# Score steps that keep a running minimum, differential values projected beside the step columns, and merged small products

## The reference, cut to what matters

```python
proj = h @ w_in[l]
a_q, a_k, a_v, b_z, b_xbc, b_dt, c_q, c_k, c_v = jnp.split(proj, offsets, axis=-1)
# windowed attention, 6 heads: softmax over scores and one sink logit per head
scores = jnp.einsum('bnqgrd,bnkgd->bngrqk', qb, kb) * (HEAD_DIM ** -0.5)
bias = -slopes * jnp.abs(rel)
scores = jnp.where(valid, scores + bias, -jnp.inf)
m = jnp.maximum(jnp.max(scores, axis=-1, keepdims=True), sink_l)
p = jnp.exp(scores - m)
denom = jnp.sum(p, axis=-1, keepdims=True) + jnp.exp(sink_l - m)
# differential attention, 4 heads of two maps each: 8 softmaxes
sc = jnp.einsum('bqhmd,bkhmd->bhmqk', qn, k) * (DIFF_QK_DIM ** -0.5)
a = jax.nn.softmax(sc - sl * dist, axis=-1)
attn = a[:, :, 0] - lam * a[:, :, 1]
# state-space mixer: b_dt goes through softplus, a running sum over tokens, and decays
dt = jax.nn.softplus(dt_raw + dt_bias)
da = jnp.cumsum(dt * a, axis=2)
y_diag = einsum(einsum(ch, bh) * decay, xdt)
```

## Time and profile before

| | before |
|---|---|
| median of 3 runs | 1211.71 us (1211.57 to 1214.07) |
| span of the profiled execution | 1213.5 us; its own time is not listed apart from the three above |
| TensorE / VectorE / ScalarE busy | 78% / 33% / 16% |
| moved by DMA | 436.64 MB, mean 360 GB/s |
| mean granted TensorE clock | 0.897 of 2.4 GHz |

### The profile page before, as it was taken

How to read it: one execution, slowest core, us unless ns; L and a number is a source line. 1 busy time by engine, 2 the same in 40 slices (tenths; PEclk the granted TensorE clock), 3 DMA queues, 4 the chain that set the end, 5 groups by cost and what they waited for, 6 DMA issues and landing times.

```text
span 1213.5 us, 26544 instructions
## 1 busy us (share of the span) xinstructions
PE 948.9 (78%) x11004; PEld 600.0 (49%) x11004; DVE 398.7 (33%) x1231; ACT 189.6 (16%) x546; POOL 8.9 (1%) x27
## 2 busy tenths in 40 slices
PE   7999989766668787895799999895666666666964
PEld 6877855433334443453387777553333333333532
DVE  4778453111122222231176774431111111111213
ACT  2245221000001110110023352110000000000101
POOL 2000000000000000000000000000000000000000
PEclk9999989888789998997899999898888888787977
DMA  9835179999999999999995244899999999999994
GB/s 342 334 123 209 70 296 425 424 427 427 426 424 424 426 426 425 400 425 428 408 394 199 97 182 156 344 426 426 425 428 426 426 427 427 425 425 426 424 423 196
DMA packets 47435, 436.64 MB, mean 360 GB/s; under 512 B 8256, under 2 KB 10304, under 8 KB 21440
## 3 DMA queue, kind: packets, MB, share of 16 engines
q1 hardware_dynamic: 47296, 434.72, 86.5%
HBM read 433.65 MB, written 1.05 MB: 358 GB/s over the span
## 4 chain that ended last, share of the span: by engine, by line
PE 47%; DMA 37%; DVE 6%; issue 5%; SPq 2%; DVEq 2%; ACT 1%; another core or an unknown queue 1%; ACTq 0%
DMA ring<-in_w_up 37%; PE ps L601 13%; PE ps L689 8%; PE ps L617 5%; PE ps L812 4%; PE ps L626 3%; PE ps L569 3%; PE ps L701 2%; PE ps L589 2%; PE ps L706 1%; PE ps L752 1%; SPq L442 1%; SPq L440 1%; PE ps L791 1%
## 5 line engine op out<-in xcount | busy, mean ns | idle before, releaser
L601 PE MATMUL ps<-ring,xg 128*32 128x256 f32 x4352 | 317.3, 455 | 176.9 <-DMA ring<-in_w_up 171.5
L601 PEld LDWEIGHTS ps<-ring,xg 128*32 128x32 f32 x4352 | 170.0, 130 | 307.3 <-issue 247.1
L1135 DVE SCALAR_TENSOR_TENSOR th<-th,ps 128x128 f32<-128x128 f32 x72 | 20.7, 288 | 593.8 <-ACT th L934 593.8
L617 PE MATMUL ps<-ring,actT 128*32 128x256 f32 x2304 | 139.2, 382 | 13.5 <-issue 12.8
L617 PEld LDWEIGHTS ps<-ring,actT 128*32 128x32 f32 x2304 | 69.0, 109 | 74.6 <-DVE actT L1139 22.3
L934 ACT ACTIVATE th<-ps 128x128 f32<-128x128 f32 x72 | 20.0, 278 | 515.7 <-PE ps L601 480.1
L569 PE MATMUL ps<-xh,Pb 128*32 128x256 f32 x1152 | 79.4, 394 | 24.5 <-issue 20.4
L689 PE MATMUL ps<-hT,ring 128*128 128x256 f32 x416 | 95.3, 386 | 0.8 <-ACT hT L971 0.8
L689 PEld LDWEIGHTS ps<-hT,ring 128*128 128x128 f32 x416 | 78.6, 193 | 12.7 <-issue 1.4
L626 PE MATMUL ps<-ysb,PwT 32*128 32x256 f32 x992 | 71.8, 403 | 0.0
L569 PEld LDWEIGHTS ps<-xh,Pb 128*32 128x32 f32 x1152 | 38.5, 113 | 49.3 <-issue 24.5
(11 more groups left out here) (251 smaller groups left out, 744.0 us busy)
## 6 DMA issues: line engine op xcount, KB each, us to landing
ring<-in_w_down SPq DMA_DIRECT2D x62, 2048.0 KB, 40.4
ring<-in_w_gate SPq DMA_DIRECT2D x60, 2048.0 KB, 45.6
ring<-in_w_up SPq DMA_DIRECT2D x60, 2048.0 KB, 47.3
ring<-in_w_in SPq DMA_DIRECT2D x6, 2048.0 KB, 19.8
ring<-in_w_out SPq DMA_DIRECT2D x4, 2048.0 KB, 19.5
ring<-in_w_gate SPq DMA_DIRECT2D x8, 1024.0 KB, 29.1
ring<-in_w_up SPq DMA_DIRECT2D x8, 1024.0 KB, 31.8
ring<-in_w_in SPq DMA_DIRECT2D x4, 1024.0 KB, 21.3
```

Source lines behind the costliest of these rows:

```text
L601: last = mm(b_gate[j * SLOTS:(j + 1) * SLOTS, 0:2 * GQ], tokens[:, k, :], ring[:, low:high + 1:high - low, o:o + GQ], start=(k == 0), stop ...
L617: last = mm(b_y[j * SLOTS:(j + 1) * SLOTS, 0:DQ], actT[:, c * SLOTS:(c + 1) * SLOTS], ring[:, slot, o:o + DQ], start=(c == 0), stop=(c == ...
```

## The change

1. **Scores.** The scale and the slope are put into the queries (`qscale`, one factor per partition, applied in the copies of `aq` and `cq`). `sc.u` on VectorE becomes two `tensor_tensor_reduce` instructions, one per 128 queries, each of which adds the distance table to the bank, multiplies by -slope and keeps the running minimum, started at the negated sink (or a large number). The exponential on ScalarE then uses scale -1 and that minimum as bias. The maxima and the scaling of them go away.
2. **Step columns beside differential values.** Input piece 1 now holds the last 128 columns of `xbc`, the 12 `dt` columns and the 256 columns of `c_v`, loaded by two DMAs; piece 4 holds `cq` and `ck`. The steps `dt` (TensorE part) and `cv` are replaced by `dc.0` and `dc.1`, one per 128 tokens, each 8 matmuls of 268 columns, placed where `dt` was. ScalarE copies them out with the norm factor; VectorE's `dt` starts from that copy.
3. **Merged products.** `cum` takes both token halves in one product, so 3 matmuls take the place of 6. `cb.0` and `cb.1` become one TensorE step `cB`, placed where `cb.0` was, whose four matmuls alternate between the two halves of the rows; ScalarE still copies `cb.0` and `cb.1` in their old places.

The bank planner runs over the new list. By its rule `pT.6` now gets bank 0 (it is the lower of two that tie), so `outA.0` waits for ScalarE's copy of `pT.6`; `outA.1` waits for VectorE's `sc.12`, and `outA.2` for `sc.10`.

```diff
-W_IN_PIECES = [(O_XBC, 512), (O_XBC + 512, O_CK - O_XBC - 512), (O_AQ, O_AV), (O_AV, O_XBC - O_AV), (O_CK, D_IN - O_CK)]
+W_IN_PIECES = [[(O_XBC, 512)], [(O_XBC + 512, O_CQ - O_XBC - 512), (O_CV, D_IN - O_CV)], [(O_AQ, O_AV)], [(O_AV, O_XBC - O_AV)],
+               [(O_CQ, O_CV - O_CQ)]]
+DC = 2 * S_H + C_H * C_V
 ORDER = """
...
-    dt conv.4 ak silu.3 aq.0 dta xs.0 silu.4 sc.0 nm.0 aq.2 xs.1 aS.0 cum cumT aq.1 lam cb.0 sc.1 sc.2 seg.0.0
+    dc.0 dc.1 dt conv.4 ak silu.3 aq.0 dta xs.0 silu.4 sc.0 nm.0 aq.2 xs.1 aS.0 cum cumT aq.1 lam cB cb.0 sc.1 sc.2 seg.0.0
...
-    pT.2 cq.1 sc.5 pT.3 y.5 sc.6 cS.0 sc.7 oa.0 nm.5 ybn pT.4 nm.6 cv oa.1 pT.5 yT.0 yT.1 oa.2 sc.8 sc.9 sc.10
+    pT.2 cq.1 sc.5 pT.3 y.5 sc.6 cS.0 sc.7 oa.0 nm.5 ybn pT.4 nm.6 oa.1 pT.5 yT.0 yT.1 oa.2 sc.8 sc.9 sc.10
     nm.7 pT.6 cS.1 sc.11 sc.12 outA.0 pT.7 outA.1 od.0 nm.8 sc.13 nm.9 pT.8 od.1 outA.2 pT.9 od.2 od.3 outA.3 ycn
...
+        return [("cb", g) for g in range(S_G)]
...
-                    elif kind == "dt":
+                    elif kind == "dc":
                         w = piece(piece_of(s), s)
+                        t = s[1]
+                        for k in range(KC):
+                            last = mm(bank[:, 0:DC], hT[:, k, t * P:(t + 1) * P], w[:, k, P:P + DC], start=(k == 0), stop=(k == KC - 1))
...
+                        sums = bank[:, 0:TT * 4 * S_H].rearrange("p (t n) -> p t n", t=TT)
+                        mm(sums[:, :, 0:S_H], upto[:, :], dta[:, :, 0:S_H], start=True, stop=True)
+                        mm(sums[:, :, S_H:2 * S_H], since[:, :], dta[:, :, S_H:2 * S_H], start=True, stop=True)
+                        last = mm(sums[:, :, 2 * S_H:4 * S_H], ones[:, :], dta[:, :, 0:2 * S_H], start=True, stop=True)
...
+                        for t in range(TT):
+                            for g in range(S_G):
+                                r = slice(g * S_N, (g + 1) * S_N)
+                                last = mm(ps[BANK["cb", g]][:, t * SEQ:(t + 1) * SEQ], xc[r, 3, t * P:(t + 1) * P], xc[r, 4, :],
+                                          start=True, stop=True)
...
+                        last = A(dcv[:, s[1], :], bank[:, 0:DC], ACT.Copy, scale=root[:, TT + s[1]:TT + s[1] + 1])
...
+                            last = A(pb[:, t, :], pb[:, t, :], ACT.Exp, bias=low[:, u, t:t + 1], scale=-1.0, accum_out=den[:, u, t:t + 1])
...
+                        dve.wait_ge(done["act"], nth(li, "act", ("dc", 0), ("dc", 1)))
+                        v.tensor_tensor(z.rearrange("p (t n) -> p t n", t=TT), dcv[:, :, 0:n],
+                                        rowp[:, R_DTB:R_DTB + n].unsqueeze(1).broadcast_to([P, TT, n]), ALU.add)
...
-                            v.scalar_tensor_tensor(pb[:, t, :], table[:, o:o + SEQ], slope, bank[:, t * SEQ:(t + 1) * SEQ],
-                                                   ALU.mult, ALU.add)
-                        dve.drain()
-                        v.reduce_max(nmx[:, 0, u, :], pb[:, :, :], AX_X)
-                        if u < A_H:
-                            dve.drain()
-                            last = v.tensor_scalar(nmx[:, 1, u, :], nmx[:, 0, u, :], -A_SCALE, nsink[:, HEAD[u]:HEAD[u] + 1],
-                                                   ALU.mult, ALU.min)
-                        else:
-                            dve.drain()
-                            last = v.tensor_scalar(nmx[:, 1, u, :], nmx[:, 0, u, :], -C_SCALE, None, ALU.mult)
+                            last = v.tensor_tensor_reduce(pb[:, t, :], bank[:, t * SEQ:(t + 1) * SEQ], table[:, o:o + SEQ], -slope, least,
+                                                          ALU.add, ALU.min, low[:, u, t:t + 1])
```

More of the change, by code:

```diff
@@ L140, in piece_of @@
         return len(W_IN_PIECES) + (kind == "outB")
-    return {"xbc": int(step[-1] == 4), "dt": 1, "cq": 1, "aq": 2, "ak": 2, "vz": 3, "ck": 4, "cv": 4}.get(kind)
+    return {"xbc": int(step[-1] == 4), "dc": 1, "aq": 2, "ak": 2, "vz": 3, "cq": 4, "ck": 4}.get(kind)
 USERS = [[step for step in COUNT["pe"] if piece_of(step) == n] for n in range(PIECES)]
@@ L687, in _ @@
                             else:
-                                lhs = w[:, k, c * P:(c + 1) * P]
+                                o = O_CK - O_CQ + c * P
+                                lhs = w[:, k, o:o + P]
                             last = mm(bank[:, 0:SEQ], lhs, hT[:, k, :], start=(k == 0), stop=(k == KC - 1))
-                    elif kind == "dt":
+                    elif kind == "dc":
                         w = piece(piece_of(s), s)
[L692 to L696, removed]
+                        t = s[1]
+                        for k in range(KC):
+                            last = mm(bank[:, 0:DC], hT[:, k, t * P:(t + 1) * P], w[:, k, P:P + DC], start=(k == 0), stop=(k == KC - 1))
                     elif kind == "vz":
@@ L701, in _ @@
                             last = mm(bank[:, :], hT[:, k, t * P:(t + 1) * P], w[:, k, :], start=(k == 0), stop=(k == KC - 1))
[L702 to L707, removed]
                     elif kind == "cum":
@@ L998, in _ @@
                         last = A(vz[:, s[1], :], bank[:, :], ACT.Copy, scale=root[:, TT + s[1]:TT + s[1] + 1])
-                    elif kind == "cv":
+                    elif kind == "dc":
                         act.wait_ge(done["dve"], nth(li, "dve", ("sq",)))
-                        for t in range(TT):
-                            last = A(cv[:, t, :], bank[:, t * C_H * C_V:(t + 1) * C_H * C_V], ACT.Copy, scale=root[:, TT + t:TT + t + 1])
+                        last = A(dcv[:, s[1], :], bank[:, 0:DC], ACT.Copy, scale=root[:, TT + s[1]:TT + s[1] + 1])
                     elif kind == "zs":
@@ L1091, in _ @@
             v = nc.vector
+            for half in range(2):
+                r = slice(half * A_D, (half + 1) * A_D)
+                for c in range(REP):
+                    v.memset(qscale[r, c:c + 1], A_SCALE / SLOPE[HEAD[A_KV * c + half]])
+                for c in range(2):
+                    v.memset(qscale[r, REP + c:REP + c + 1], C_SCALE / SLOPE[A_H + 2 * c + half])
             dve.wait_ge(x_loaded, 16)
@@ L1201, in _ @@
                               "aq": lambda c: aqT[:, c, :], "ak": lambda: akT[:, :], "ck": lambda c: ckT[:, c, :]}[kind](*s[1:])
-                        last = v.tensor_tensor(to, bank[:, 0:SEQ], root_row[:, :], ALU.mult)
+                        if kind in ("aq", "cq"):
+                            q0 = s[1] + (REP if kind == "cq" else 0)
+                            last = v.scalar_tensor_tensor(to, bank[:, 0:SEQ], qscale[:, q0:q0 + 1], root_row[:, :], ALU.mult, ALU.mult)
+                        else:
+                            last = v.tensor_tensor(to, bank[:, 0:SEQ], root_row[:, :], ALU.mult)
                     elif kind == "dt":
```

62 lines of the change are left out of this document (29 added, 33 removed).

## The result

| | before | after |
|---|---|---|
| median of 4 runs each, us | 1212.89 (1211.57 to 1215.15) | 1237.08 (1235.36 to 1238.19) |
| ratio, 95% interval | | 1.0196 [1.0176, 1.0216] |
| span of the profiled execution, us | 1213.5 | 1233.5 (its own time 1235.36) |

The change costs 24.2 us. The forecast was 1231 us, slower; the sum was +19 us.

A forecast was written before the change was run, and what follows sets the result against it. It took the experts as DMA-bound and mixers as paid one to one, bound by TensorE up to `cq.1`, then by TensorE, VectorE and ScalarE in turn. Waits of 5.7 plus dips of 3.7 us per layer gave 1231 us, range 1215 to 1240.

The forecast's parts named there:

- the sum: Both mixers: 5.7 us of lateness plus 3.7 us of clock dips, 9.4 us per layer, 19 us in all.
- score pass: VectorE's new score instruction on 256 columns, priced at 0.42 us, between 0.35 and 0.70 us.
- The saving that counts for nothing: Mixer up to `cS.1`: 5.0 us less TensorE work per layer is worth nothing, as VectorE's chain takes the gap.
- The bank plan: Waits for `pT.6` and `sc.12`: `outA.0` starts 3.7 us late, `outA.1` and the mixer's end 5.7 us late.
- The clock: TensorE at 1.2 GHz: 1.2 us over `yT` to `cS.1`, 1.7 at `outA.0`, 0.8 at `outA.1`; 3.7 us per layer.
- The mixers together: Both mixers end late by 5.7 us of waits and 3.7 us of clock each, 19 us for both.
- The first (the clock holds): Rival: same mixer waits but TensorE keeps its clock; 11.4 us slower in all, 1223 us; chance 0.15.
- The second: Rival: TensorE's saving after `cq.1` counts in full, `outA.0` starts before 111.2 us; 1202 us; chance of faster 0.06.
- The third (the slow instruction): Rival: the new score instruction takes 0.70 us, a score step 1.5 us; 5.4 us more, 1236 us; chance 0.12.
- The range: From 1215 us (waits at two thirds, short `dc`, no dips) to 1240 us (slow scores, full clock price on one layer).
- The step that was wrong all the same: Experts: they need the same bytes after a late mixer, so each microsecond in a mixer moves the end equally.

The follow-up runs named there:

- e12: After, with banks 0 and 1 kept free from `pT.6` on, plus 11 products of 12 columns before `oa.1` and 8 of 256 before `yT.0`: 1207.13 us.
- e8: Before, with one unused 4-byte-per-partition tile ahead of the weight ring and nothing else: 1206.64 us, ratio 0.9944.
- e1: After, with the bank planner keeping banks 0 and 1 free from `pT.6` until `outA`: 1219.33 us, ratio 1.0047 to before.
- e2: Before, with only two waits added: `outA.0` also waits for the copy of `pT.6`, `outA.1` for `sc.12`: 1244.13 us, ratio 1.026.
- e5: After, with useless 256-column products per layer: 10 before `yT.0`, 8 before `outA.0`, 4 before `outA.1`: 1217.47 us, ratio 1.0037 to before.
- e9: After, with 19 useless 12-column products (38 instructions) per layer before `yT.0`: 1229.22 us, ratio 1.0137 to before.

## Why the prediction was right, and what it left out

**The steps in the mixer.** All start times of layer 0 were reckoned from the profiled execution of before; in after everything lies 1.7 us earlier for want of the early dip (29.68 against 31.36). With that taken off the start times:

| step | forecast, less 1.7 us | measured |
|---|---|---|
| `dc`, us | 7.3 to 7.5 | 7.23 |
| score pass, us | 0.42 | 0.42 |
| end of `cq.1` | 97.3 | 96.95 |
| `nm.5` starts | 103.3 | 102.88 |
| `sc.8` starts | 113.05 | 112.66 |
| `outA.0` starts, with 1.2 us for the clock | 119.35 | 119.39 |
| `outA.1` starts, with 1.7 us more | 128.9 to 129.0 | 128.69 |

- *The saving that counts for nothing.* Right. 5.0 us of TensorE work per layer went, and e12 against e8 shows that in all none of it reached the end.
- *The bank plan.* Right, and it is the main cause: freeing two banks gives 17.7 us back (e1), adding the two waits to before costs 31 us (e2). e5 has the same waits without the dips: `outA.1` is 6.0 us late, forecast 5.7, the late `cq.1` and the gap before `yT` included.
- *The clock.* The mechanism is shown, both by the rows and by e5. The size was near: 9.6 us for two layers, or 7.9 without the dip before `outB`, which the forecast had in before and after alike; forecast 7.4. The dips came at `yT`, `outA.0` and `outA.1` as listed; in layer 0 both `outA` were hit where I had given the second even chances, in layer 1 the first took 8.49 us. The old dip before `outB` is there again in layer 0 (8.87 us) and absent in layer 1 (7.19), which took 1.7 us off my sum.
- *The mixers together.* Forecast 18.8 us; measured +9.1 and +8.0 to the first expert product, +10.1 and +8.3 to the end of `outB`.
- *Rivals.* The first (the clock holds) is excluded by the clock rows. The second is excluded for this kernel: `outA.0` started at 119.39, not before 111.2. The third (the slow instruction) is excluded by the 0.42 us rows; the running minimum costs nothing over the plain pass of L1322. With the sink as a start value in a tile the pass takes 0.48 us, in `sc.0` to `sc.5`, where it matters little.
- *The range.* Its lower end does not come out of the terms named for it: two thirds of 3.7 and 2.0 us without dips are 3.8 us per layer, which gives 1219 us, not 1215.

**The step that was wrong all the same.** I wrote that the experts then need all the bytes they needed before, so that a microsecond in a mixer moves the end by the same. The second half holds (e2). The first half was taken to mean that the expert stretches stay as they are, and they didn't:
- The ring's new address: -6.6 us, shown by e8 and by the rate in the rows, up to the tiles behind the ring. I had set the `qscale` writes at nothing and never asked where that tile pushes the others.
- Two further gather waits in layer 0: 10 to 12 us. The experts of layer 0 take 451.5 us against 439.2 in e9 and 441.0 in e8. The idle time before the gathers is 8.7 us longer than in e8 and 9.1 longer than in e9; for the rest I have no cause.

So 17.1 us of mixers and 4.6 us of experts (about +11 and -6.5) make 21.7 of the 24.2 us; the rest lies within the distance of the profiled executions from their medians. The number was near partly by luck: the two omitted terms took half of each other away. Without the -6.6 the time would have been about 1244 us, outside the range.

**What stays open.** Why a program with fewer TensorE instructions ahead of the experts meets more waits for a block of instructions. The fourteen kernels, one of them with a never-executed block, exclude the time of arrival and the mere size of the program. But the products that raise the count also push the experts' code further on in the program, by the same number, so the count and the place of that code in its blocks of 16384 B were not told apart. Nor do the traces say why TensorE stands for about 3 us more after the block has landed, or whether a still larger count brings the waits back.

## What to carry to other kernels

When a change reorders or quickens steps, rerun the buffer or bank assignment in your head for the steps next in line: a tie broken the other way cost more here (17.7 us) than the 10 us of TensorE work that the change takes away. Work that hides in a gap keeps TensorE's clock up as well; before taking it away, look at what stands in its place and at what that work was filler for. And compare the bulk stretches too, their GB/s and their unexplained idle time, since a 4-byte tile ahead of a large buffer was worth 6.6 us and three useless products per layer 3.6.

## What the runs showed of the hardware that was not expected

- Rows of 16384 B are written at 429 GB/s to slots that begin at a multiple of 256 B in SBUF, and at 426 GB/s to slots 192 B past one (e8: -6.6 us of 1213).
- TensorE waits 6.2 to 7.2 us before some gathers while a block of 16384 B of instructions is loaded; it lands 2.8 to 3.1 us before TensorE goes on (42 waits in 14 traces). 38 fewer matmul instructions per layer brought two more waits in layer 0 (after against e9).
- The clock fell to 1.2 GHz in the midst of an unbroken run of 12-column products before `yT.0` (e9, 0.63 at 108 to 112 us); with 256-column ones before `yT.0` and both `outA` it was at 2.4 GHz from 112 us on (e5).
- A combined add, scale and running minimum over 256 float32 from PSUM and SBUF takes 0.42 us plus a read of 0.08 us, and the pass is no longer than the plain one; with a start value from a tile it takes 0.48 us:

```profile
L1335 DVE CUSTOM_DVE_ANT_0 pbuf<-ps,dist 128x256 f32<-128x256 f32 x16 | 6.2, 423 | 18.3 <-PE ps L776 16.7 <-PE ps L768 1.3 <-issue 0.2
L1335 DVE CUSTOM_DVE_ANT_0 pbuf<-ps,distw,nsink 128x256 f32<-128x256 f32 x12 | 5.3, 482 | 2.1 <-PE ps L761 1.3 <-issue 0.6
```
